# Two chained sequence-model blocks on one Trainium2 core: full tile shapes and two small projections as small tiles, with the first units and the start of the second block reworked

## The chip, the core and the metric

One core of a Trainium2 chip runs the whole program in one launch. The metric is device time in microseconds (us), the median of several executions. TensorE (PE) multiplies, VectorE (DVE), ScalarE (ACT) and GpSimd (POOL) work elementwise, and SyncE (SP) issues the DMA transfers. All data is float32. "fp32r" is float32 rounded so that the TensorE takes it in one pass; a plain float32 matmul is taken in two passes and shows as two records in the trace.

## The reference

The input x has 256 tokens of width 1024. It goes through two blocks, one behind the other.

```python
def first_block(x, ...):
    h = rmsnorm(x, mix_pre_norm[l])
    u = h @ w_in[l]
    u_z, u_xbc, u_dt, u_ly, u_lx, u_g = jnp.split(u, list(IN_SPLITS), axis=-1)
    y_a = ssd_mixer(u_z, u_xbc, u_dt, ...)      # Mamba-2, 16 heads; u_dt has 16 columns
    y_b = rglru_mixer(u_ly, u_lx, ...)
    g = jax.nn.sigmoid(u_g.reshape(b, s, N_BRANCHES, D_MODEL) + gate_b[l])
    merged = g[:, :, 0, :] * (y_a @ w_proj_ssm[l]) + g[:, :, 1, :] * (y_b @ w_proj_lru[l])
    x = x + rmsnorm(merged @ w_out[l], mix_post_norm[l])
    h = rmsnorm(x, ffn_pre_norm[l])
    up = causal_dwconv(h @ w_ffn_up[l], ffn_conv_w[l], ffn_conv_b[l])
    f_gate, f_val = jnp.split(up, 2, axis=-1)
    f = (jax.nn.gelu(f_gate, approximate=True) * f_val) @ w_ffn_down[l]
    return x + rmsnorm(f, ffn_post_norm[l])

def _layer(x, mem, ...):                        # the second block
    h = _rmsnorm(x, norm_pre)
    cols = h @ w_in
    (dn_qkv, dn_z, dn_b, dn_a, gm_uv, gm_z, sw_q, sw_k, sw_v, sw_z,
     xm_q, xm_z, gate_logits) = _split_cols(cols)   # dn_b and dn_a have 4 columns each
    mem_kv = _rmsnorm(mem, norm_mem) @ w_mem_kv
    y_a = _deltanet_branch(dn_qkv, dn_z, dn_b, dn_a, ...)
    y_b = _spatial_gating_branch(gm_uv, gm_z, ...)
    y_c = _sliding_window_branch(sw_q, sw_k, sw_v, sw_z, sinks)   # 8 heads of 64, 2 key heads
    y_m = _memory_branch(xm_q, xm_z, mem_kv)
    ...
    merged = jnp.sum(gates * proj, axis=2)
    return x + _rmsnorm(merged @ w_out, norm_post)
```

## The kernel before

**Weights.** Each weight is streamed from memory in 260 units of 128x1024 (512 KB), in the order of the list that `stream` builds. SP fetches a unit into one of NR = 5 raw buffers. ACT copies it, rounded, to WH (`split` in the ACT program, L1230). DVE makes the rest, WL = raw - WH (L1741). There are NS = 4 pairs of WH and WL. The activations are split in the same way into a high part (Hh, or YBh) and a low part (Hl, or YBl). PE does three products for each 128x128 piece of a weight: high by high, high by low, low by high (`three`, L605 to L607). The names t_wh, t_wl, t_hh, t_hl and t_br in the trace are these buffers (t_br holds YBh and YBl in turn with other data), and L610 (`mm`) is every other matmul.

**Chunks.** `chunk` (L625) multiplies 256 columns of a weight, two units with 24 matmuls of 256 tokens each. `turned` and `four` keep the tokens on the partitions, and write 512 weight columns with one matmul. `chunk_by_k` goes over the 8 parts of the activations one at a time and waits for each.

**Order.** Every engine's program walks through the same units (`Walk`, L194). At each unit a tick goes by, at which the side work, called lanes, is stepped on: the scan of the SSD branch, the recurrence, the chain of the second block's deltanet (`dn_lane`), its sliding window (`sw_lane`), and others. A lane waits with `walk.until(t)` for a tick out of a table such as T_SW (L301). So the order on each engine is fixed, and a late operation holds up what stands behind it. `bank_table` (L251) says which of the 8 PSUM banks each chunk writes.

**Start.** SP fetches unit 0, the parameters (par), x in four pieces, the constants (con), units 1 to 4, then masks and block matrices (bd). ACT makes the high part of x times the norm's weight (YBh), and DVE the low part (YBl). PE begins with "dt", a chunk of 128 columns of which 16 are wanted, then sums the squares of x over the partitions with a column of ones (`column_sums`, L715), then xbc4, the spread of the norm over the partitions (`norm_spread`), and xbc5. These run on x before the norm; g0 and xbc0 behind them need the normed Hh and Hl.

**Between the blocks.** The last column tile of the first block's FFN (j = 23) passes ACT, then a rounded copy of it is made and its low part on POOL (L2454). Its matmuls are the last ones of the down projection. `sqrt_table` (L1270) loads another set of ACT's functions. Chunks mk2 and mk3 of the memory's keys and values run on PE while the FFN's output is normed, turned by PE (`tr`, L613) and split again. The second block's units begin with "dn_ba", a chunk of 128 columns of which 8 are wanted, and dnq.

**Sliding window.** For each of 4 x 2 steps a visit to PE makes the scores S (a mask in bf16, then queries by keys, on tiles of 64 rows by 64 heads' channels), and a later one the output o (probabilities by values, 64 output columns). The visits stand between the 512-wide matmuls of the gates' chunks.

## Time and profile before

| what | value |
| --- | --- |
| runs | 869.72, 871.77, 869.59 us |
| median | 869.72 us |
| the profiled execution's own time | 871.67 us |
| its span in the trace | 869.8 us |
| granted TensorE clock, mean | 0.995 |
| busy: PE, DVE, ACT, POOL | 848.3, 624.1, 509.0, 78.4 us |
| DMA | 149.21 MB, mean 172 GB/s |

The span runs from the first to the last event in the trace; the profiled execution took 1.87 us more than its span. The median of the runs is 1.95 us under the profiled execution. "Busy" counts the time in which an engine had an instruction in work. PEld is the loading of weights into the TensorE, which overlaps its matmuls.

### The profile page before, as it was taken

How to read it: one execution, taken by the hardware profiler on the slowest of the kernel's cores; microseconds unless marked ns; L12 is line 12 of the kernel's file. 1: busy time of each engine (PE TensorE's matmuls, PEld its weight loads, DVE VectorE, ACT ScalarE, POOL GpSimd, SP SyncE). 2: the span in 40 equal slices, each digit the busy share in tenths (PEclk: the TensorE clock that was granted, in tenths of full speed). 3: DMA queues.
4: the chain of work that ended last, by engine and by line, in shares of the span. 5: the costliest groups of instructions: out<-in, count | busy, mean ns of one | idle time of the engine just before them, and what ended most of it. 6: DMA issues, size and time to landing. Idle time of an engine off the chain costs nothing.

```text
span 869.8 us, 14548 instructions
## 1 busy us (share of the span) xinstructions
PE 848.3 (98%) x5760; PEld 776.0 (89%) x5760; DVE 624.1 (72%) x1124; ACT 509.0 (59%) x826; POOL 78.4 (9%) x83
## 2 busy tenths in 40 slices
PE   5999999999999999999999999999999999999997
PEld 5999999899989999999998799899899887778885
DVE  6787987988868766666665979777555467775765
ACT  5655778665367755555656787554544445544453
POOL 0200001201020111111112100500000100000000
PEclk9999999999999999999999999999999999999999
DMA  9457443466454655555554463844322243365541
GB/s 342 140 190 286 160 140 119 150 211 256 155 199 150 238 188 194 174 182 202 176 194 169 146 198 124 308 147 146 97 98 97 98 145 122 125 213 191 196 145 49
DMA packets 40588, 149.21 MB, mean 172 GB/s; under 512 B 4524, under 2 KB 4680, under 8 KB 39880
## 3 DMA queue, kind: packets, MB, share of 16 engines
q1 hardware_dynamic: 40520, 148.27, 50.2%
q8 instruction: 46, 0.75, 0.3%
q14 instruction: 22, 0.18, 0.1%
HBM read 147.18 MB, written 1.08 MB: 170 GB/s over the span
## 4 chain that ended last, share of the span: by engine, by line
PE 87%; DVE 7%; ACT 3%; issue 2%; DMA 1%; SPq 0%; DVEq 0%; ACTq 0%
PE bank L610 39%; PE bank L605 16%; PE bank L607 15%; PE bank L606 15%; PE bank L613 2%; DVE t_wl L1741 2%; DVE t_arena L1756 1%; DVE t_arena L1746 1%; ACT t_arena L1235 1%; DVE t_x L1756 1%; ACT t_hh L1235 1%; DMA t_x<-in_xin 1%; ACT t_wh L1230 1%; DVE t_sm L1753 1%; ACT t_br L1235 0%
## 5 line engine op out<-in xcount | busy, mean ns | idle before, releaser
L1741 DVE TENSOR_TENSOR t_wl<-t_raw,t_wh 128x1024 fp32r<-128x1024 f32 x260 | 316.6, 1226 | 112.1 <-ACT t_wh L1230 111.0
L1230 ACT ACTIVATE t_wh<-t_raw 128x1024 fp32r<-128x1024 f32 x260 | 273.4, 1058 | 128.3 <-PE bank L610 60.6
L605 PE MATMUL bank<-t_hh,t_wh 128*128 128x256 f32 x1144 | 330.3, 289 | 2.9 <-DVE t_hl L1746 1.5
L607 PE MATMUL bank<-t_hh,t_wl 128*128 128x256 f32 x1144 | 323.5, 283 | 0.0
L606 PE MATMUL bank<-t_hl,t_wh 128*128 128x256 f32 x1144 | 323.5, 283 | 0.0
L605 PEld LDWEIGHTS bank<-t_hh,t_wh 128*128 128x128 f32 x1144 | 219.1, 192 | 6.8 <-issue 4.2
L606 PEld LDWEIGHTS bank<-t_hl,t_wh 128*128 128x128 f32 x1144 | 219.2, 192 | 0.8
L607 PEld LDWEIGHTS bank<-t_hh,t_wl 128*128 128x128 f32 x1144 | 219.1, 191 | 0.0
L610 PE MATMUL bank<-t_wh,t_br 128*128 128x512 f32 x384 | 123.5, 392 | 0.2 <-POOL t_br L2454 0.2
L1756 DVE SCALAR_TENSOR_TENSOR t_arena<-bank,t_par,t_arena 128x255 f32<-128x255 f32 (+2 forms) x184 | 75.2, 474 | 45.0 <-ACT t_arena L1235 44.7
L610 PE MATMUL bank<-t_wh,t_hh 128*128 128x512 f32 x224 | 91.9, 410 | 1.8 <-DVE t_wl L1741 1.8
L610 PE MATMUL bank<-t_wh,t_hl 128*128 128x512 f32 x224 | 88.3, 394 | 0.0
L610 PE MATMUL bank<-t_wl,t_hh 128*128 128x512 f32 x224 | 88.2, 394 | 0.0
L610 PEld LDWEIGHTS bank<-t_wh,t_br 128*128 128x128 f32 x384 | 72.2, 188 | 16.2 <-issue 1.6
L1235 ACT ACTIVATE t_arena<-bank 128x512 f32<-128x512 f32 (+4 forms) x75 | 42.2, 575 | 62.0 <-PE bank L610 35.5
L610 PE MATMUL bank<-t_wl,t_br 128*128 128x512 f32 x192 | 74.9, 390 | 0.0
L2454 POOL TENSOR_TENSOR t_br<-t_arena,t_br 128x256 fp32r<-128x256 f32 x30 | 34.5, 1154 | 307.5 <-ACT t_br L1235 307.5
L1235 ACT ACTIVATE t_arena<-bank,t_par 128x256 f32<-128x256 f32 x76 | 37.6, 547 | 39.3 <-PE bank L607 39.3
L610 PE MATMUL bank<-t_arena 128*128 128x128 f32 (+5 forms) x360 | 54.5, 298 | 0.8 <-DVE t_arena L1746 0.8
L610 PEld LDWEIGHTS bank<-t_wh,t_hh 128*128 128x128 f32 x224 | 42.5, 190 | 12.6 <-DVE t_wl L1741 2.5
L610 PEld LDWEIGHTS bank<-t_arena 128*128 128x128 f32 (+2 forms) x360 | 45.2, 185 | 6.8 <-issue 2.9
L610 PEld LDWEIGHTS bank<-t_wh,t_hl 128*128 128x128 f32 x224 | 42.5, 190 | 9.4
(154 smaller groups left out, 850.3 us busy)
## 6 DMA issues: line engine op xcount, KB each, us to landing
t_raw<-in_ws SPq DMA_DIRECT2D x260, 512.0 KB, 3.9
t_br<-decay SPq DMA_DIRECT2D x1, 2048.0 KB, 8.4
t_arena<-in_post SPq DMA_DIRECT2D x3, 512.0 KB, 4.9
t_arena<-gates SPq DMA_DIRECT2D x1, 1536.0 KB, 10.6
t_x<-in_xin SPq DMA_DIRECT2D x4, 256.0 KB, 5.9
t_bd<-in_bd SPq DMA_DIRECT2D x1, 1024.0 KB, 11.6
t_x<-in_xtok SPq DMA_DIRECT2D x1, 1024.0 KB, 5.8
t_arena<-in_mem SPq DMA_DIRECT2D x1, 1024.0 KB, 8.1
```

The lines of the kernel that those rows point to most:

```text
L605: e.matmul(o, wh, xh, start=first, stop=False, skip_group_check=True)
L606: e.matmul(o, wh, xl, start=False, stop=False, skip_group_check=True)
L607: return e.matmul(o, wl, xh, start=False, stop=last, skip_group_check=True)
L610: return e.matmul(o, l, r, start=st, stop=sp, skip_group_check=True)
L613: return e.transpose(o, i, ident[0:i.shape[0], 0:i.shape[0]])
L1230: e.activation(WH[q % NS][:, :], RAW[q % NR][:, :], ACT.Copy, bias=0.0, scale=1.0).then_inc(*hi.now(q))
L1235: return e.activation(o, i, f, bias=bias, scale=scale)
L1741: e.tensor_tensor(WL[q % NS][:, :], RAW[q % NR][:, :], WH[q % NS][:, :].bitcast(F), SUB).then_inc(*lo.now(q))
L1746: return e.tensor_tensor(o, a, b, op)
L1753: return e.tensor_scalar(o, a, s1, s2, op0, op1)
L1756: return e.scalar_tensor_tensor(out=o, in0=a, scalar=s, in1=b, op0=op0, op1=op1)
L2454: return e.tensor_tensor(o, a, b, op)
```

## The change

- "dt" and "dn_ba" leave the stream, which has two units fewer. Their wanted columns come as small tiles by transfers of their own (`first`, with the first norm's weights, and `gates`). The tile holds high and low weights side by side, 32 columns for dt and 16 for the gates, so each of the 8 parts takes two matmuls: 16 in place of 24, on 32 or 16 columns in place of 128.
- At the start SP issues `first`, x in two pieces, unit 0, the first 280 columns of con, unit 1, par, and then the units; what is left of con, the masks and bd come at units 6, 10 and 12. Constants that POOL made now come from the host. PE runs 5 float32 matmuls on zeros before its first data.
- The squares of x are added on DVE to one tile (two more additions), and so are those of mem and of the SSD's output (two tiles to one in each group). The column sums take 4 records in place of 16 for x and for mem, and 8 in place of 16 for the SSD. Those of x stand inside xbc4, the spread inside xbc5. The root of the first norm comes from ACT with a Newton step on DVE, not from DVE's integer code. g0 is taken unit by unit.
- The chunks pl0 to pl3 wait for each quarter of YB where they need it, no longer for the whole of it ahead of pl0.
- For j = 23 the low part is made on DVE, and `sqrt_table` stands behind the high copy. The FFN's output is turned by tiles of 128 tokens (`turn_tile`), vu's four units come first in the second block, by tiles of tokens, then the small gates tile, then dnq. The deltanet's lane starts 4 to 5 ticks later.
- In the sliding window the keys are laid into a tile with zeros (SWK2, cleared by POOL), so that S uses all 128 rows, and o is made for both key heads at once, on 128 output columns.

The core of the diff:

```diff
-    s.append(("dt", "w_in", rng(DTC, 128)))
...
         s.append((f"dnq{i}", "w_in_2", rng(DNQ + 256 * i, 256)))
-    for n in range(2):
-        for i in range(2):
-            s.append((("vu", "vv")[n] + str(i), "moving", ("w_in_2", i, rng(GMU + 512 * n, 512))))
+    for i in range(2):
+        s.append((f"vv{i}", "moving", ("w_in_2", i, rng(GMU + 512, 512))))
     for i in range(2):
         s.append((f"xmq{i}", "w_in_2", rng(XMQ + 256 * i, 256)))
     for i in range(2):
...
+        SWQt, SWK2 = ar(12, 4, T), ar(58, 2, T)
...
 
+            e.dma_start(DTW, first).then_inc(s_first, 16)
+            for i in range(2):
+                e.dma_start(X[:, 4 * i:4 * i + 4, :], xin[:, 4 * i:4 * i + 4, :]).then_inc(s_x[i], 16)
             fetch(0)
+            e.dma_start(conT[:, 0:NFIRST], con[:, 0:NFIRST]).then_inc(s_con, 16)
+            fetch(1)
             e.dma_start(parT[:, :], par).then_inc(s_par, 16)
-            for i in range(4):
-                e.dma_start(X[:, 2 * i:2 * i + 2, :], xin[:, 2 * i:2 * i + 2, :]).then_inc(s_x[i], 16)
-            e.dma_start(conT[:, :], con).then_inc(s_con, 16)
-            for q in range(1, NR):
+            for q in range(2, NR):
...
-            e.dma_start(MSK, masks).then_inc(s_msk, 16)
-            e.dma_start(bdT[:, :, :], bd).then_inc(s_bd, 16)
             for q in range(NR, NU):
+                if q == 6:
...
+            def turn_tile(tt):
+
+                e.wait_ge(*a_ns.of("scaled", "pre2", tt, 0))
+                e.wait_ge(*d_ns.of("scaled", "pre2", tt, 1))
+                if tt == 0:
+                    for b in (0, 3):
+                        bank_free(("turn", "pre2", b))
+                for k in range(8):
+                    m = tr(PB[TILE_BANK[tt][k // 4]][:, 128 * (k % 4):128 * (k % 4) + 128], XS[:, tt, 128 * k:128 * k + 128])
+                m.then_inc(*p_ht.now("pre2", tt))
+
...
+            def mix_sums():
+                e.wait_ge(s_con, 16)
+                e.wait_ge(*d_add.of("mix", 3))
+                column_sums(7, 0, [SC0[:, 0, :]], True, True).then_inc(*p_norm.now("mix", "sum"))
...
-                    m = column_sums(3, 2 * g, [SSQ[:, 4 * g + k, :] for k in range(2)], g == 0, g == 1)
+                    m = column_sums(3, 2 * g, [SSQ[:, 4 * g, :]], g == 0, g == 1)
...
+                    kt, q = SWK2[:, a_, :], SWQt[:, i, :]
                     yield from walk.until(T_SW[n][0])
...
-                    mm(o[:, 0:T], SWV_[:, 0, r], pt[:, 0:T], True, False)
-                    mm(o[:, 128:T], SWV_[:, 1, r], pt[:, T:384], False, True).then_inc(*p_sw.now("o", i, a_))
+                    mm(PB[6][:, 0:T], SWV_[:, 0, :], pt[:, 0:T], True, False)
+                    mm(PB[6][:, 128:T], SWV_[:, 1, :], pt[:, T:384], False, True).then_inc(*p_sw.now("o", i, a_))
                 yield
 
...
-            chunk_by_k("dt", YBh, YBl, x_weighted)
-            e.wait_ge(s_con, 16)
-            norm_sums_first("mix", 7, SC0)
-            norm_sums_last("mix", 7, SC0)
-            chunk("xbc4", YBh, YBl)
-            norm_spread("mix", 7)
-            chunk("xbc5", YBh, YBl)
+            e.wait_ge(*d_const.of("warm"))
+            for _ in range(5):
+                mm(PB[3][:, 0:T], SC1[:, 0, 0:128], SC1[:, 0, :])
+            e.wait_ge(*d_dt.of("w"))
+            for k in range(8):
+                e.wait_ge(*d_xw.of(k))
+                mm(PB[6][0:32, 0:T], DTS[:, k, :], YBh[:, k, :], k == 0, False)
+                m = mm(PB[6][0:16, 0:T], DTS[:, k, 0:16], YBl[:, k, :], False, k == 7)
+            m.then_inc(*p_dt.now("dt"))
+            chunk("xbc4", YBh, YBl, {(1, 4): mix_sums})
...
-                    chunk_by_k("g0", Hh, Hl, normed("mix"))
-                    e.wait_ge(*d_f.of("mix", 7))
+                    chunk_by_units("g0", Hh, Hl, normed("mix"))
...
 
 
-            e.wait_ge(*d_yb.of(3))
+            def hidden(q):
+                return lambda: e.wait_ge(*d_yb.of(q))
+
             for i in range(4):
-                chunk(f"pl{i}", YBh, YBl)
...
-            norm_sums_first("mem", 3, MEMQ)
-            norm_sums_last("mem", 3, MEMQ)
+            mem_sums()
...
-                    e.wait_ge(*g_fl.of(20 + i))
+                    e.wait_ge(*(d_fp.of("low") if i == 3 else g_fl.of(20 + i)))
...
-                        turn_rows("pre2", 0)()
+                        turn_tile(0)
                     for tt in range(2):
-                        if i == 1 and j == 1 and tt == 1:
...
-            chunk_by_k("dn_ba", Hh, Hl, normed("pre2"))
+            turn_tile(1)
+            us = walk.four(4)
+            for tt in range(2):
+                for i, u in enumerate(us):
+                    if tt == 0:
+                        split_ready(u)
+                    e.wait_ge(*d_hl.of("pre2", tt, 2 * i + 1))
+                    m = turned(f"vu{i // 2}", u, 2 * i, Hh, Hl, i == 0, i == 3, (tt,))
+                    if tt == 1:
+                        m.then_inc(*unit.now(u))
+                if tt == 0:
+                    m.then_inc(*p_tok.now("vu1"))
+            e.wait_ge(*d_rw.of("w"))
+            e.wait_ge(*a_ev.of("free", "vu", 0))
+            for k in range(8):
+                mm(PB[6][0:16, 0:T], BAS[:, k, :], Hh[:, k, :], k == 0, False)
+                m = mm(PB[6][0:8, 0:T], BAS[:, k, 0:8], Hl[:, k, :], False, k == 7)
+            m.then_inc(*p_rw.now("ba"))
...
@@ -1274,11 +1343,47 @@
                 e.wait_ge(*d_ns.of(tag, tt, "rs"))
                 act(XS[:, tt, halves(0)], XT[:, tt, halves(0)], ACT.Copy, scale=row_stats(1, tt)[1]).then_inc(*a_ns.now("scaled", tag, tt, 0))
 
+            def tile_parts(tt, ks):
+                for k in ks:
+                    act(Hh[:, k, 128 * tt:128 * tt + 128], PB[TILE_BANK[tt][k // 4]][:, 128 * (k % 4):128 * (k % 4) + 128], ACT.Copy,
+                        scale=pc("pre2", k)).then_inc(*a_hh.now("pre2", tt, k))
+
+            def second_norm(q):
...
+                e.wait_ge(*p_ht.of(pre, 0))
+                tile_parts(0, range(6))
+                walk.ahead(q + 6)
+                chunk_done("mk3")
+                e.wait_ge(*d_hl.of(pre, 0, 5))
+                tile_parts(0, (6, 7))
+                walk.ahead(q + 7)
+                e.wait_ge(*p_ht.of(pre, 1))
+                tile_parts(1, range(8))
+                act(BAS[:, :, 0:8], BAW, ACT.Copy).then_inc(*a_rw.now("w"))
+
             def token_norm(post, pre, q, between):
...
                     act(cg, cg, ACT.Gelu_apprx_tanh).then_inc(*a_fg.now(j))
-                    if j == 23:
-                        sqrt_table()
...
                     elif j == 0:
                         chunk_done("wo1_1")
                     act(YBh[:, j % 8, :], FF[:, j % 2, :], ACT.Copy).then_inc(*a_fh.now(j))
+                    if j == 23:
+                        sqrt_table()
                 for i in range(6):
...
+                act(YBh[:, k, :], X[:, k, :], ACT.Copy, scale=WMIX[:, k:k + 1]).then_inc(*a_xw.now(k))
             split(0)
-            walk.split_to = 1
-            e.wait_ge(s_par, 16)
-            for k in range(8):
-                if k % 2 == 0:
-                    e.wait_ge(s_x[k // 2], 16)
-                act(YBh[:, k, :], X[:, k, :], ACT.Copy, scale=pc("mixpre", k)).then_inc(*a_xw.now(k))
...
+                yield from walk.until(T_FU[23] + 2)
+                e.wait_ge(*a_fh.of(23))
+                tt(YBl[:, 7, :], FF[:, 1, :], YBh[:, 7, :].bitcast(F), SUB).then_inc(*d_fp.now("low"))
...
-                       ADD).then_inc(*d_ssd.now("gsum", g))
+                       ADD).then_inc(*d_ssd.now("gsums", g))
+                    e.wait_ge(*d_ssd.of("gsums", g))
+                    tt(SSQ[:, 4 * g, :], SSQ[:, 4 * g, :], SSQ[:, 4 * g + 1, :], ADD).then_inc(*d_ssd.now("gsum", g))
...
 
-            split(0)
-            walk.split_to = 1
+            e.memset(SM[:, 392:393], 1.0).then_inc(*d_const.now("one"))
+            e.memset(SC1[:, 0, :], 0.0).then_inc(*d_const.now("warm"))
...
+            e.wait_ge(*d_add.of("mix", 1))
+            tt(SC0[:, 0:2, :], SC0[:, 0:2, :], SC0[:, 6:8, :], ADD).then_inc(*d_add.now("mix", 2))
+            e.wait_ge(*d_add.of("mix", 2))
+            tt(SC0[:, 0, :], SC0[:, 0, :], SC0[:, 1, :], ADD).then_inc(*d_add.now("mix", 3))
+            walk.split_to = 2
+            walk.unit(2)
+            o, v, r, t, h = NW[:, 0, 0:2], NW[:, 1, 0:2], NW[:, 2, 0:2], NW[:, 2, 2:4], NW[:, 1, 2:4]
+            e.wait_ge(*p_norm.of("mix", "sum"))
+            ts(v, PB[7][:, 0:2], 1.0 / 1024, MUL, EPS, ADD).then_inc(*d_rs.now("mix", "v"))
+            e.wait_ge(*d_rs.of("mix", "v"))
```

What stands on PE at the start before (t_br is YBh or YBl, the three rows of a part repeat eight times, then the column sums and xbc4):

```order
L605 MATMUL bank<-t_br,t_wh 128x256
L606 MATMUL bank<-t_br,t_wh 128x256
L607 MATMUL bank<-t_br,t_wl 128x256
```

And what stands there now, of which the second and third row repeat eight times:

```order
L630 MATMUL bank<-t_arena 128x256 x5
L630 MATMUL bank<-t_br,t_wh 32x256
L630 MATMUL bank<-t_br,t_wh 16x256
```

The five matmuls on zeros and 16 narrow ones took the place of 24 full ones, and xbc4 follows them at once.

On ACT at the end of the first block's FFN, before (t_br is the high part of j = 23, t_hh x4 the second half of a norm, L1230 the split of a unit):

```order
L1235 ACTIVATE t_arena<-t_arena 128x256
L1235 ACT_TABLE_LOAD
L1235 ACTIVATE t_sm<-t_con 128x1
L1235 ACTIVATE t_br<-t_arena 128x256
L1235 ACTIVATE t_hh<-t_arena 128x512 x4
L1230 ACTIVATE t_wh<-t_raw 128x1024
L1256 ACTIVATE t_arena,t_sm<-bank 128x512 x2
```

The same place now:

```order
L1304 ACTIVATE t_arena<-t_arena 128x256
L1304 ACTIVATE t_br<-t_arena 128x256
L1304 ACT_TABLE_LOAD
L1304 ACTIVATE t_sm<-t_con 128x1
L1304 ACTIVATE t_hh<-t_arena 128x512 x4
L1299 ACTIVATE t_wh<-t_raw 128x1024
L1325 ACTIVATE t_arena,t_sm<-bank 128x512 x2
```

The table load moved behind the copy of j = 23's high part; the rest of the row order is kept.

On PE in a visit of the sliding window, o and a part of the deltanet's work, before (t_pw is the tile of values):

```order
L610 MATMUL bank<-t_arena 128x128 x4
L610 MATMUL bank<-t_px,t_arena 128x256 x2
L610 MATMUL bank<-t_pw,t_arena 64x256
L610 MATMUL bank<-t_pw,t_arena 64x128
L605 MATMUL bank<-t_hh,t_wh 128x256
```

And now:

```order
L630 MATMUL bank<-t_arena 128x128 x4
L630 MATMUL bank<-t_px,t_arena 128x256 x2
L630 MATMUL bank<-t_pw,t_arena 128x256
L630 MATMUL bank<-t_pw,t_arena 128x128
L625 MATMUL bank<-t_hh,t_wh 128x256
```

Nothing moved here; the two matmuls write 128 columns in place of 64.

## Rows read from the trace of the kernel before

**Rows 1.** The page: span, and busy time of each engine.

```profile
span 869.8 us, 14548 instructions
PE 848.3 (98%) x5760; PEld 776.0 (89%) x5760; DVE 624.1 (72%) x1124; ACT 509.0 (59%) x826; POOL 78.4 (9%) x83
```

**Rows 2.** PE's waits: line, releaser, us in total, times, longest.

```profile
PE bank L605 <- DVE t_br L1756: 8.5, 1, 8.5
PE bank L610 <- DVE t_wl L1741: 1.8, 1, 1.8
```

**Rows 3.** Windows: length, PE, PEld, DVE, ACT, POOL, clock, DMA share, GB/s.

```profile
8.53:11.70 3.17, 3.17 (x15) 3.17 (x16) 2.65 (x7) 3.17 (x9) 0.00 (x0) 1.00 1.01 376
15.07:18.50 3.43, 3.43 (x18) 3.43 (x18) 3.29 (x10) 1.58 (x2) 0.00 (x0) 0.51 1.01 418
489.24:493.00 3.76, 3.76 (x10) 2.98 (x11) 3.51 (x12) 3.26 (x5) 0.00 (x0) 0.55 0.42 139
```

**Rows 4.** Timeline of ACT and DVE at the start: start, duration, instruction, wait.

```profile
4.67 1.06 ACT L1230 ACTIVATE t_wh<-t_raw 128x1024 fp32r<-128x1024 f32 x1 [2.66 <-DMA t_raw<-in_ws]
7.36 3.30 ACT L1235 ACTIVATE t_br<-t_x,t_par 128x256 fp32r<-128x256 f32 x8 [1.64 <-DMA t_x<-in_xin]
7.90 3.27 DVE L1756 SCALAR_TENSOR_TENSOR t_br<-t_x,t_par,t_br 128x256 fp32r<-128x256 f32 x8 [0.92 <-ACT t_br L1235]
```

**Rows 5.** Timeline of PE from the column sums to g0.

```profile
13.29 1.92 PE L610 MATMUL bank<-t_con,t_arena 128*128 128x1 f32 x16 [0.25 <-DVE t_arena L1746]
15.07 0.53 PE L605 MATMUL bank<-t_br,t_wh 128*128 128x256 f32 x1
...
30.68 0.36 PE L605 MATMUL bank<-t_hh,t_wh 128*128 128x256 f32 x1 [1.50 <-DVE t_hl L1746]
```

**Rows 6.** Timeline of PE, a visit with full 128-row tiles.

```profile
102.17 0.28 PE L607 MATMUL bank<-t_hh,t_wl 128*128 128x256 f32 x1
102.29 1.03 PE L610 MATMUL bank<-t_arena,t_bd 128*128 128x256 f32 x4
103.27 0.28 PE L606 MATMUL bank<-t_hl,t_wh 128*128 128x256 f32 x1
```

**Rows 7.** Timeline of PE, a visit of the SSD lane with 64-column tiles.

```profile
132.56 0.88 PE L610 MATMUL bank<-t_x,t_arena 128*64 128x256 f32 x8
```

**Rows 8.** Timeline of PE, the sliding window's o and S visits.

```profile
734.20 0.39 PE L610 MATMUL bank<-t_wh,t_hl 128*128 128x512 f32 x1
734.52 0.86 PE L610 MATMUL bank<-t_pw,t_arena 128*64 128x256 f32 x4
735.65 0.40 PE L610 MATMUL bank<-t_wl,t_hh 128*128 128x512 f32 x1
...
737.75 0.39 PE L610 MATMUL bank<-t_wl,t_hh 128*128 128x512 f32 x1
737.98 0.39 PE L610 MATMUL bank<-t_wh,t_hl 128*128 128x512 f32 x1
...
738.48 0.92 PE L610 MATMUL bank<-t_arena 64*128 64x128 f32 x4
...
739.66 0.40 PE L610 MATMUL bank<-t_wl,t_hh 128*128 128x512 f32 x1
```

**Rows 9.** Timeline of PE, pl0's first matmul, and the column sums of mem.

```profile
190.54 0.39 PE L605 MATMUL bank<-t_br,t_wh 128*128 128x256 f32 x1 [0.32 <-DVE t_br L1746]
...
222.09 1.84 PE L610 MATMUL bank<-t_con,t_arena 128*128 128x1 f32 x16
```

**Rows 10.** Timeline between the blocks, ACT, DVE and PE.

```profile
473.34 1.28 ACT L1235 ACT_TABLE_LOAD   x1
...
475.08 2.18 ACT L1235 ACTIVATE t_hh<-t_arena 128x512 fp32r<-128x512 f32 x4
...
487.97 1.22 DVE L1741 TENSOR_TENSOR t_wl<-t_raw,t_wh 128x1024 fp32r<-128x1024 f32 x1
...
489.24 0.53 PE L610 MATMUL bank<-t_wh,t_hh 128*128 128x512 f32 x1 [1.82 <-DVE t_wl L1741]
```

More of the change, by code:

```diff
@@ L326, in dn_bank, with build_program @@
     return 3 + (DN_AT[name] + 1) % 3
-def build_program(nc, ws, par, con, masks, bd, rows, swt, xin, xtok, min_, post, decay, gates2, out):
+def build_program(nc, first, gates, ws, par, con, masks, bd, rows, swt, xin, xtok, min_, post, decay, gates2, out):
     ctx = ExitStack()
@@ L641, in chunk, with chunk_by_units @@
                     walk.tick()
+            def chunk_by_units(name, xh, xl, x_ready):
+                b = BANK[name]
+                for j in range(2):
+                    q = walk.unit(NS - 1 - j)
+                    wh, wl = weights(q, 8)
+                    split_ready(q)
+                    if j == 0:
+                        bank_free(name)
+                    for k in range(8):
+                        if j == 0:
+                            x_ready(k)
+                        m = three(half(b, j), wh[:, k, :], wl[:, k, :], xh[:, k, :], xl[:, k, :], k == 0, k == 7)
+                    m.then_inc(*unit.now(q))
             def chunk_by_k(name, xh, xl, x_ready):
@@ L1630, in act_program @@
                 act(MV[:, tt, :], PB[BANK["mv", tt]][:, :], ACT.Copy).then_inc(*a_ev.now("free", "mv", tt))
-            walk.cols("dn_ba", True)
+            walk.four(4)
+            for tk in range(2):
+                e.wait_ge(*tokens_done("vu1", tk))
+                act(GU[:, tk, :], PB[BANK["vu", tk]][:, :], ACT.Gelu_apprx_tanh).then_inc(*a_ev.now("free", "vu", tk))
+                walk.ahead(FIRST["dnq0"] + 2)
             for i in range(6):
@@ L1669, in act_program @@
             chunk_done("swkv")
-            act(SWK_[:, 0, :], half(BANK["swkv"], 0), ACT.Copy)
+            e.wait_ge(*g_dn.of("pads"))
+            for a in range(2):
+                act(SWK2[64 * a:64 * a + 64, a, :], half(BANK["swkv"], 0)[64 * a:64 * a + 64, :], ACT.Copy)
             act(SWVt[:, 0, :], half(BANK["swkv"], 1), ACT.Copy).then_inc(*a_ev.now("swkv"))
@@ L2279, in dve_program @@
-            square_adds("mix", SC0)
-            walk.cols("dt", True)
-            rsqrt("mix", NW, 7, 2, 1024, p_norm.of("mix", "sum"))
-            walk.cols("xbc4")
-            e.wait_ge(*p_norm.of("mix", "row"))
+                stt(YBl[:, k, :], X[:, k, :], WMIX[:, k:k + 1], YBh[:, k, :].bitcast(F), MUL, SUB).then_inc(*d_xw.now(k))
+            split(0)
+            e.wait_ge(*a_sq.of("mix", 1))
+            tt(SC0[:, 0:2, :], SC0[:, 0:2, :], SC0[:, 2:4, :], ADD).then_inc(*d_add.now("mix", 0))
@@ new lines, in dve_program @@
+            walk.split_to = 2
+            walk.unit(2)
+            o, v, r, t, h = NW[:, 0, 0:2], NW[:, 1, 0:2], NW[:, 2, 0:2], NW[:, 2, 2:4], NW[:, 1, 2:4]
+            e.wait_ge(*p_norm.of("mix", "sum"))
+            ts(v, PB[7][:, 0:2], 1.0 / 1024, MUL, EPS, ADD).then_inc(*d_rs.now("mix", "v"))
+            e.wait_ge(*d_rs.of("mix", "v"))
+            ts(h, v, -0.5, MUL).then_inc(*d_rs.now("mix", "half"))
+            e.wait_ge(*a_sq.of("mix", "root"))
+            e.reciprocal(o, r).then_inc(*d_rs.now("mix", "guess"))
@@ L2284, in dve_program @@
+            e.wait_ge(*d_rs.last())
+            tt(t, o, o, MUL).then_inc(*d_rs.now("mix", "oo"))
+            e.wait_ge(*d_rs.last())
+            tt(t, t, h, MUL).then_inc(*d_rs.now("mix", "t"))
+            e.wait_ge(*d_rs.last())
+            stt(o, t, 1.5, o, ADD, MUL).then_inc(*d_rs.now("mix"))
+            walk.tick()
+            walk.unit(2)
+            walk.tick()
+            walk.unit(1)
+            walk.tick()
+            h_parts("mix", SC1, X, WMIX, 7, {4: 4})
             e.tensor_copy(ROWR, PB[7][:, 0:T]).then_inc(*d_const.now("row"))
-            walk.cols("xbc5")
@@ L2286, in dve_program @@
-            h_parts("mix", SC1, X, "mixpre", 7)
+            e.wait_ge(s_par, 16)
+            walk.unit()
+            walk.tick()
             ts(hbr, pc("br", 0, 8), 0.5, MUL)
@@ L2370, in dve_program @@
             walk.four(3)
[L2371 removed]
+            second_norm(FIRST["mk2"])
             walk.cols("mk2", True)
             walk.cols("mk3")
[L2376 removed]
+            walk.four(4)
             for i in range(6):
@@ L2548, in pool_program @@
             walk.tick()
-            walk.cols("pl0")
-            block_masks()
-            for i in range(1, 4):
+            for i in range(4):
                 walk.cols(f"pl{i}")
@@ L2572, in pool_program @@
             walk.cols("mk3")
-            walk.cols("dn_ba", True)
+            walk.four(4)
             for name in MIDDLE:
```

361 lines of the change are left out of this document (222 added, 139 removed).

## The prediction

> **What bounds the kernel now.** I read the page first. PE has an instruction in work for 848.3 of 869.8 us, DVE for 624.1 and ACT for 509.0 [rows 1], so the time is PE's instructions one behind the other, and an edit is worth what it takes off PE or off PE's few waits. The list of PE's waits comes next: one of 8.5 us before the first matmul and one of 1.8 us at a t_wl are the largest [rows 2]; the timeline shows 1.50 us ahead of g0 [rows 5] and 0.32 us at pl0 [rows 9]. Then the windows: the granted clock is 0.51 from 15.07 to 18.50 us and 0.55 from 489.24 to 493.00, the 1.2 GHz level, and 1.00 elsewhere. The engine worked through the 6.5 us before the first of these and stood still before the second [rows 3]. In 3.43 us at 0.51 PE got through 18 matmuls, 0.19 us each. At full clock a matmul on 256 columns follows the last after 0.12 us (102.17 to 102.29 [rows 6]) and one on 512 columns after 0.23 us (737.75 to 737.98 [rows 8]). These are the prices of the sum.
>
> **Part A, the start.** Before, ACT splits unit 0 at 4.67, waits 1.64 us for x, and makes YBh in 3.30 us, 0.41 us for each of the 8 parts; the low parts on DVE end half a microsecond later (11.17) [rows 4]. The dt matmuls run from 8.53 and are done at about 13; the sums of squares follow, and xbc4 starts at 15.07 [rows 5]. After, x is no longer queued behind unit 0 and par. Half a megabyte at 376 to 418 GB/s [rows 3] takes 1.3 us, so x comes some 1.5 to 2 us earlier, and YBh starts at about 5.5. It ends at 5.5 + 3.3 = 8.8, the split of unit 0 at 8.8 + 1.06 = 9.9, and DVE's part of it at 9.9 + 1.22 = 11.1; with the squares' additions between, I put xbc4 at 11.5. The 16 narrow dt matmuls keep ACT's pace and are done before. The matmuls on zeros run while PE would wait.
>
> xbc4 has 48 matmuls (48 x 0.12 = 5.8 us) and now 4 records of column sums (rows 9 give 1.84 / 16 = 0.115 us for a record, so 0.5): it ends at 17.7. xbc5 takes 5.8 and the spread 0.4, so PE could begin g0 at 23.9. The norm must be through by then. Its sums stand in xbc4 three quarters of the way, at about 16; root, reciprocal and Newton step are some ten small operations, the spread follows, and the normed parts can begin at about 19.8. Hh and Hl are made at 0.4 to 0.5 us a part, with two splits between: about 24.0. So the 1.50 us wait goes. In its second unit g0 waits for DVE, which has Hl and the splits queued, about 0.9 us. g0 ends at 24.0 + 5.8 + 0.9 + 0.4 = 31.1, where before it ended at 30.68 + 5.8 = 36.5. That is 5.4 us. DVE then stands closer to PE than before: its work up to unit 20 is the same and PE is 5 us nearer, so I give back 0.9 to 2.5 us and take **-3.7 us** (bounds -5.5 and -2.5; if a stretch at 1.2 GHz falls into xbc4 as it does now, it costs 1.7 us as it did).
>
> **Part B, sums and small waits.** For mem 12 records go and for the SSD's groups 8, 20 x 0.115 = 2.3 us on PE's path. In exchange DVE gets additions of 256 columns that lie beside PE's work. pl0's wait of 0.32 us [rows 9] goes, since its first matmuls need only a quarter of YB. Together **-2.6 us** (bounds -2.0 and -3.0, the low one if DVE's additions push pl0's later quarters).
>
> **Part C, full shapes in the sliding window.** From 734.20 to 735.65 lie two 512-wide intervals and one o visit: 1.45 - 2 x 0.23 = 0.99 us. From 737.98 to 739.66 likewise 1.68 - 0.46 = 1.22 us for an S visit [rows 8]. What a visit with full tiles costs stands at 102.17 to 103.27: 1.10 - 2 x 0.12 = 0.86 us for two matmuls of 256 columns, four records, and nothing beyond them, 0.215 a record [rows 6]. The o visit has 256 and 128 columns in two passes, 3 x 0.215 = 0.65: it saves 0.34. The S visit has the same two and a mask of 384 bf16 columns (0.23 x 384 / 512 = 0.17): 0.82, it saves 0.40. Eight of each are 8 x 0.74 = 5.9; two o visits share their place with other narrow tiles, which keeps a tenth: **-5.8 us** (bounds -4.5 and -6.3). The price of cleared keys (a POOL write) and of one more copy on ACT lies far from PE's path: both engines are idle for much of the span.
>
> What the saving rests on is that a narrow tile brings a cost around it, and that narrow tiles do not overlap each other. The SSD lane's visit speaks against the second: eight records on 64 columns in 0.88 us [rows 7], as long as four in the o visit at 0.86 [rows 8], so pairs on different columns ran side by side there. In the sliding window the two matmuls of a step use one tile, one after the other, and nothing stands beside them; so the full shape gives up no overlap. The Trainium skill says the same of the cost around ("TensorEngine Tiling (Array Packing)", Key Properties: "Mode switching requires drain"). But another of its rules speaks against the edit: "TensorE: Matmul & The Clock Gate", Part 3, has small tiles run concurrently, and advises slicing them so. By that rule alone the 64-row tiles were no slower than full ones, and part C would be 0.
>
> **Part D, the start of the second block.** What goes: dn_ba, 24 x 0.12 = 2.9 us and a short wait and pacing around it, 0.4 together. What comes: 16 narrow matmuls, 16 x 0.115 = 1.8, and a visit's extra of 0.34 as in part C. Net -1.1 us. vu's four units only move. The chain on ACT that ends at the first matmul of the second block is made longer. The table load of 1.28 us stays ahead of the four Hh copies (2.18 us) [rows 10], it only passes behind j = 23's high copy, which PE needs: PE is done with the FFN earlier and then waits for mk2 and mk3 that much longer, a gain of nothing. For mk3 the split at 487.97 must still be done before PE goes on at 489.24 [rows 10]. New are 16 copies by halves of the tokens in place of 8, and the cast of the gates' tile, some 1.5 us on ACT, of which vu on the first tile hides part only. I take +1.6 for these, and **D = +0.5 us** (bounds -2 and +3.5; a stretch at 1.2 GHz more or less is 1.7 us either way, which is what 489.24 to 493.00 costs now: 3.76 x 0.45 [rows 3]). The deltanet's lane starts 4 to 5 ticks later; it had some 16 ticks to spare before its output is wanted, so I cost it at nothing. What covers it are the gates' chunks. Without that cover, each tick is a unit of some 2.8 us.
>
> **Sum.** -3.7 - 2.6 - 5.8 + 0.5 = -11.6. Against the profiled execution's 871.67 us this is 860.1; the median of the runs is 1.95 lower, which gives 858.1. I say **858.2 us**, and its own range is 854 to 862.
>
> **The rivals.**
> 1. The start brings little: the work on DVE up to unit 20 decides, not PE's order. For it: at 0.51 clock DVE was busy 3.29 of 3.43 us [rows 3]. Against: masks, bd and 24 matmuls do leave the start. Then A is -1 and the time 861.
> 2. The second block's start loses: two more waits of 1.5 us, and a second stretch at 0.55. D is +3.5 and the time 861.
> 3. Full shapes bring nothing, either by the rule of concurrent tiles or because the 0.3 us around a narrow visit belongs to any float32 visit. Against: the visit at 102 us [rows 6] is such a one and has nothing around it. The time is 864.
> 4. On the other side: the deltanet's chain becomes what PE waits for. It is fixed in order; if it comes 5 ticks late and its slack is gone, PE's waits are those of its steps, about 45 visits x 0.3 us = 13.5 us, less the 11.6, so 871.6 on the median. It decides from 11.6 us on. For it: the lane was moved. Against: PE waits 1.1 us in two places for t_arena in all, so nothing is near the edge today.
> 5. Both the start and the second block gain in full, and no stretch at 1.2 GHz falls into xbc4 or vu: A -5.5, D -2, 853.
>
> **How the numbers follow.** The forecast 0.62, rival 1 0.12, rival 2 0.12, rival 3 0.07, rival 4 0.02, rival 5 0.05. The range 853.5 to 863.5 holds the forecast and rivals 1 and 2 with their neighbours and leaves out most of 3 to 5. 0.3% is 2.6 us, about what a measurement tells from no change. Faster takes all but rival 4 and a part of mixed mishaps: 0.95; the same 0.03; slower 0.02.
>
> **What would show it.** In the changed kernel's timeline: xbc4 at about 11.5 and g0 at about 24 with no wait ahead of it, xbc0 at about 31; column sums of 4 records; o visits of 0.65 us and S visits of 0.82 between 512-wide matmuls; at pl0 no wait; in the windows the stretches at half clock; ahead of vu waits of 1 to 2 us for a split or an Hl. I am wrong if the visits keep 0.99 and 1.22 us, if DVE sets the first 50 us, or if PE's waits for t_arena grow over some microseconds.

## The result, and the profile after

The changed kernel took 863.94 us in the median (863.07 to 866.02, 4 runs), the kernel before 870.55 us beside it. The ratio is 0.9927, with a 95% interval of 0.9902 to 0.9952: 0.5 to 1.0% faster. The forecast was 858.2 us with a range of 853.5 to 863.5. The direction holds, the gain is 6.6 us where 11.6 were worked out, and the median lies just above the range.

The page of the changed kernel:

```profile
span 864.2 us, 14493 instructions
PE 840.4 (97%) x5726; PEld 772.3 (89%) x5726; DVE 625.4 (72%) x1130; ACT 510.9 (59%) x839; POOL 72.8 (8%) x76
```

PE's busy time fell by 7.9 us against [rows 1], although 4.0 us of matmuls on zeros are new in it; the span fell by 5.6. The list of PE's waits answers to [rows 2]:

```profile
PE bank L633 <- DVE t_arena L1871: 3.3, 2, 1.7
PE bank L630 <- DVE t_wl L1866: 3.2, 2, 1.6
PE bank L625 <- DVE t_wl L1866: 2.6, 4, 1.4
PE bank L630 <- DVE t_px L1881: 2.4, 1, 2.4
PE bank L630 <- DVE t_arena L1871: 1.7, 1, 1.7
PE bank L630 <- DVE t_br L1881: 1.4, 1, 1.4
```

The wait of 8.5 us at the start is down to 1.4, since PE now has its matmuls on zeros there (1.2 us of waiting stand ahead of them and 1.4 us ahead of xbc4); but t_arena and t_px stand for 3.3 + 2.4 + 1.7 = 7.4 us in four places, where the kernel before had one wait above a quarter of a microsecond of this kind (0.8). The timeline of PE from the start to the middle (start, duration, instruction, wait):

```profile
1.21 3.99 PE L630 MATMUL bank<-t_arena 128*128 128x256 f32 x10 [1.21 <-DVE t_arena L2439]
11.12 0.51 PE L625 MATMUL bank<-t_br,t_wh 128*128 128x256 f32 x1 [1.43 <-DVE t_wl L1866]
48.97 0.39 PE L625 MATMUL bank<-t_hh,t_wh 128*128 128x256 f32 x1 [0.35 <-DVE t_wl L1866]
216.34 0.50 PE L630 MATMUL bank<-t_con,t_arena 128*128 128x1 f32 x4
483.37 0.51 PE L630 MATMUL bank<-t_wh,t_hh 128*128 128x512 f32 x1 [1.64 <-DVE t_wl L1866]
```

The place at 48.97 is this one of the kernel before:

```profile
52.97 0.38 PE L605 MATMUL bank<-t_hh,t_wh 128*128 128x256 f32 x1 [0.36 <-DVE t_wl L1741]
```

So the start is worth 4.0 us. xbc4 starts at 11.12, 3.95 us sooner than in [rows 5]. At the column sums of mem the lead is 222.09 - 216.34 = 5.75 us, against [rows 9], and behind them 7.1, since 4 records stand for 16. At mk3 it is 489.24 - 483.37 = 5.9 us, against [rows 10]: 1.2 us were lost between the blocks. The four visits in which PE now waits:

```profile
568.33 0.45 PE L630 MATMUL bank<-t_px,t_arena 128*128 128x256 f32 x1 [2.36 <-DVE t_px L1881]
662.69 0.55 PE L633 MATMUL bank<-t_con,t_arena 128*128 128x128 f32 x3 [1.66 <-DVE t_arena L1871]
684.72 0.49 PE L630 MATMUL bank<-t_arena 128*128 128x128 f32 x2 [1.72 <-DVE t_arena L1871]
756.57 0.66 PE L633 MATMUL bank<-t_con,t_arena 128*128 128x128 f32 x4 [1.60 <-DVE t_arena L1871]
```

The first is the spatial gating's product at tick 171, the others are the deltanet's transposes at tick 193, its product at 197, and its last transposes at 214. Of the first one's 2.36 us about 1 us belongs to this one execution: in the traces of `xm1`, `table_back` and `no_warm` below, whose edits lie elsewhere, that wait is 1.41, 1.44 and 1.39 us, so the four are 6.4 us without it. A fifth, of 0.86 us at 637 us for ACT, is new as well and stands for the 0.8 that went. What DVE does ahead of the second of the four:

```profile
652.64 0.17 DVE L1877 TENSOR_SCALAR t_sm<-t_sm 128x2 f32<-128x2 f32 x1
656.59 0.17 DVE L2392 RECIPROCAL t_sm<-t_sm 128x2 f32<-128x2 f32 x1 [3.77 <-ACT t_px L1583]
...
657.32 0.61 DVE L2418 TENSOR_REDUCE t_sm<-bank 128x1 f32<-128x128 f32 x2
657.97 0.23 DVE L1878 TENSOR_SCALAR t_sm<-t_sm 128x2 f32<-128x2 f32 x1
659.36 0.16 DVE L1871 TENSOR_TENSOR t_sm<-t_sm 128x2 f32<-128x2 f32 x1 [1.16 <-ACT t_sm L1304]
...
660.82 1.21 DVE L1866 TENSOR_TENSOR t_wl<-t_raw,t_wh 128x1024 fp32r<-128x1024 f32 x1
661.96 1.27 DVE L1871 TENSOR_TENSOR t_arena<-t_arena,bank 128x512 f32<-128x512 f32 x2
```

This is tick 191: the softmax of the memory attention's last head (t_px) and one of the sliding window (t_pw) stand one behind the other, each with a wait for ACT's exponential, then a unit's low part, and only then the sum (t_arena) for which PE waits. Between 652.64 and 661.96 us DVE waited twice, for 3.77 and 1.16 us, so it was not short of time. What held PE up was the order of the work. The longer wait goes back to PE itself, by way of ACT: the exponential stands on ACT behind a copy of the deltanet's product, and that copy waited for PE:

```profile
655.05 0.60 ACT L1304 ACTIVATE t_arena<-bank 128x512 f32<-128x512 f32 x1 [3.40 <-PE bank L630]
```

In the kernel before, ACT has done the deltanet's copies by then (from 665.26 us), and DVE's wait at the same softmax is 1.09 us.

The windows that answer to [rows 3], the first columns as there:

```profile
11.12:14.58 3.46, 3.46 (x16) 3.46 (x17) 3.16 (x5) 2.66 (x4) 0.00 (x0) 0.52 1.06 414
483.37:487.00 3.63, 3.63 (x19) 3.04 (x20) 3.42 (x13) 2.80 (x5) 0.00 (x0) 1.00 0.49 158
```

In this execution the stretch at the lower clock near the start is still there, and the one at 489 us is gone.

### The profile page after: what moved, and what is told of

Read it like the earlier page. It is cut to its first block and busy times, and to the rows that moved or that the text cites. A ratio compares the mean times of both kernels' runs of the same rounds, so it can differ in the third digit from the quotient of the medians.

```text
span 864.2 us, 14493 instructions
## 1 busy us (share of the span) xinstructions
PE 840.4 (97%) x5726; PEld 772.3 (89%) x5726; DVE 625.4 (72%) x1130; ACT 510.9 (59%) x839; POOL 72.8 (8%) x76
## 5 line engine op out<-in xcount | busy, mean ns | idle before, releaser
L1304 ACT ACTIVATE t_arena<-bank 128x512 f32<-128x512 f32 (+5 forms) x76 | 42.7, 572 | 54.5 <-PE bank L630 35.5
L630 PE MATMUL bank<-t_arena 128*128 128x128 f32 (+4 forms) x370 | 57.7, 304 | 2.9 <-DVE t_arena L1871 1.7
L630 PEld LDWEIGHTS bank<-t_arena 128*128 128x128 f32 (+2 forms) x370 | 48.8, 189 | 8.3 <-DVE t_arena L1871 2.1
```

The costliest lines, as they stand in the source:

```text
L630: return e.matmul(o, l, r, start=st, stop=sp, skip_group_check=True)
L1304: return e.activation(o, i, f, bias=bias, scale=scale)
```

## The experiments

Each ratio is to the kernel before, run beside it. Times that are compared with the changed kernel's 863.94 were measured apart from it and are good to about 1 us: the kernel before, run beside each, moved between 869.65 and 871.51 us. Where a trace shows the same thing, its number stands beside.

**The sliding window's shapes, alone and undone.** `sw_only` is the kernel before with

```diff
-                    kt, q = SWK_[r, 0, :], SWQt[r, i, :]
+                    kt, q = SWK2[:, a_, :], SWQt[:, i, :]
...
-                    mm(o[:, 0:T], SWV_[:, 0, r], pt[:, 0:T], True, False)
-                    mm(o[:, 128:T], SWV_[:, 1, r], pt[:, T:384], False, True)
+                    mm(PB[6][:, 0:T], SWV_[:, 0, :], pt[:, 0:T], True, False)
+                    mm(PB[6][:, 128:T], SWV_[:, 1, :], pt[:, T:384], False, True)
```

and the cleared SWK2; `sw_undone` is the changed kernel with the reverse.

> The kernel before with the full shapes in the sliding window and nothing else of the change. If the visits are worth what the prediction priced (8 x 0.34 and 8 x 0.40 us), the span falls by 5 to 6 us, to about 864. If the saved time only turns into waits for DVE behind it (PE arrives sooner, DVE does not), it falls by less than 3 us and new waits of 1 us and more show between 600 and 790 us.

> The changed kernel with the narrow tiles (64 rows in S, 64 columns in o) put back. If the new waits at about 565, 661, 683 and 755 us come from where the deltanet's steps stand, all four stay and the span grows by 5 to 6 us. If they come from the faster sliding window, the three after 600 us shrink and the span grows by less than 3 us.

Measured: `sw_only` 866.33 us, ratio 0.9946 (0.9930 to 0.9963), 5.2 us faster than its 871.51 beside it. `sw_undone` 869.41, 5.5 us above the changed kernel (4.5 by the ratios, 0.9979 against 0.9927), and with all four waits. The first is 1.46 us, as in the other traces with this program, the second and third 1.66 and 1.73 as there, and the last is 0.65 where it was 1.60. An o visit and an S visit of the changed kernel, in the timeline of PE:

```profile
741.77 0.39 PE L630 MATMUL bank<-t_wh,t_br 128*128 128x512 f32 x1
742.00 0.81 PE L630 MATMUL bank<-t_pw,t_arena 128*128 128x256 f32 x4
742.57 0.47 PE L630 MATMUL bank<-t_wh,t_br 128*128 128x512 f32 x1
742.88 0.39 PE L630 MATMUL bank<-t_wl,t_br 128*128 128x512 f32 x1
...
745.17 0.39 PE L630 MATMUL bank<-t_wh,t_br 128*128 128x512 f32 x1
745.40 0.34 PE L630 MATMUL bank<-t_maskW,t_identB 128*128 128x384 bf16 x1
745.58 0.82 PE L630 MATMUL bank<-t_arena 128*128 128x128 f32 x4
...
746.47 0.40 PE L630 MATMUL bank<-t_wl,t_hh 128*128 128x512 f32 x1
```

The o visit with its two neighbours takes 742.88 - 741.77 = 1.11 us, where [rows 8] have 1.45: 0.34 saved. The S visit takes 746.47 - 745.17 = 1.30, where [rows 8] have 1.68: 0.38. Part C was priced rightly, and its gain comes through in both surroundings. Three of the four waits are not the faster window's. Of the last one 0.95 us is: it is 0.65 and 0.66 us with the narrow tiles (`sw_undone`, `shift_only`) and 1.60 with the full ones, so in the changed kernel about 1 us of what the visits save is given back there.

**The deltanet's lane one tick earlier.** `dn4` is the changed kernel with every tick of that lane from 185 on lowered by 1 (185 + 3 * level to 184 + 3 * level, and so on, on all engines), `dn4_gm` the same with

```diff
-                    yield from walk.until(171 + gp)
+                    yield from walk.until(172 + gp)
```

> The changed kernel with the deltanet's steps from tick 185 on one tick earlier, so that the whole lane stands 4 ticks later than before, not 5; the sliding window and the memory attention have a pattern of 4 ticks. Theory of the phase (a step's addition on DVE falls behind both softmaxes of the same tick): the waits at about 661, 683 and 755 us go, some 4 to 5 us, span about 860 where the changed kernel's was 864.2. Theory of the load (DVE has too much in this stretch, wherever it stands): waits come back elsewhere and the span changes by less than 1.5 us. The wait at 566 us stays in both.

> As the last one, and the spatial gating's two matmul steps one tick later (172, 173). Theory: the wait of 2.4 us at 568 us is PE at tick 171 waiting for a norm that DVE begins at tick 169 behind the deltanet's transposed values, which the change moved there; a tick is 2.9 us of PE's work, so the wait goes and the span falls by a further 2 us and more, to about 858. If DVE is simply late there, the wait only moves by a tick.

Measured: `dn4` 867.98 us (0.9971, 0.9956 to 0.9985), `dn4_gm` 867.65. Both are some 4 us slower than the changed kernel. The theory of the phase fell: the three waits went, but two larger ones came. The list of PE's waits of `dn4`:

```profile
PE bank L630 <- DVE t_arena L1871: 3.6, 1, 3.6
PE bank L633 <- DVE t_arena L1871: 3.0, 1, 3.0
```

and a window behind the first of them, where the clock fell as well:

```profile
661.48:665.00 3.52, 3.52 (x18) 3.30 (x19) 1.68 (x2) 0.60 (x1) 0.00 (x0) 0.67 0.62 193
```

Behind the second, from 753.48 to 757.00 us, it was 0.69. The waits grew by 1.6 us on balance (6.6 for the 5.0 that went), and these stretches are a further part of the 4 us. Of the theory stays what its timeline shows: DVE's work of tick 191 is the same two softmaxes, and the step that has its due time next behind them waits. With the lane 5 ticks late it is the sum for tick 193; with 4 it is the masked copy for tick 193, which DVE makes behind the softmaxes; before the change the next step was due two ticks later. The spatial gating's wait went in `dn4_gm`, as expected.

**The double tick parted.** `xm1` moves only the memory attention's last head:

```diff
-T_XM = [(175, 177, 182), (183, 185, 186), (187, 189, 190), (191, 193, 194)]
+T_XM = [(175, 177, 182), (183, 185, 186), (187, 189, 190), (192, 194, 195)]
```

> The changed kernel with the memory attention's last head one tick later (192, 194, 195), the deltanet left where it is. At tick 191 DVE does the softmax of that head and one of the sliding window; in this theory, whatever step of the deltanet is due on PE soonest behind that tick waits for it (before the change that step came two ticks later). Expected: the wait at about 661 us (1.8 us) goes, the other three stay, span down by 1 to 2 us. If DVE's load and not the double tick makes it, the wait stays, since the same work stands between.

Measured: 862.75 us (0.9918, 0.9904 to 0.9933), 1.2 us under the changed kernel. In its trace the wait at 662 us is gone, the one at 684 us is 2.06 us in place of 1.72, and the other two stay. The same work in another order takes the wait away.

**Four places loosened.** `sp2` is the changed kernel with

```diff
-T_SW = [(179, 181, 190)] + [(191 + 4 * n, 193 + 4 * n, 194 + 4 * n) for n in range(7)]
+T_SW = [(179, 181, 190)] + [(192 + 4 * n, 194 + 4 * n, 195 + 4 * n) for n in range(7)]
...
-                    yield from walk.until(193 + 3 * n)
+                    yield from walk.until(193 + 4 * n)
...
-                yield from walk.until(214)
+                yield from walk.until(216)
...
-                    yield from walk.until(171 + gp)
+                    yield from walk.until(172 + gp)
```

where the deltanet's ticks between 193 and 214 go with the second line (194 and 195 + 4 * n, then 200, 203, 204).

> The changed kernel with four places loosened: the spatial gating's matmuls one tick later, the sliding window from its second step one tick later, the deltanet from the second of its two block steps one tick later, and its last transposes a tick later still. If the missing 8 us are waits between lanes that meet on DVE at a tick, all four go and the span is about 857 (864.2 less 6 to 8). If DVE is short of time there, waits of the same sum show up at other steps, and the span falls by less than 2 us.

Measured: 856.82 us (0.9854, 0.9840 to 0.9869), 7.1 us under the changed kernel, and 6.4 by the ratios (0.9927 less 0.9854), which is what the four waits sum to in the other traces (1.4 + 1.66 + 1.72 + 1.60). PE's waits on L1871 and t_px are no longer in its list, though the deltanet's lane ends a tick or two later still:

```profile
PE bank L630 <- DVE t_wl L1866: 3.2, 2, 1.6
PE bank L625 <- DVE t_wl L1866: 2.6, 4, 1.4
PE bank L630 <- DVE t_arena L2439: 1.2, 1, 1.2
```

**The lane's shift alone.** `shift_only` is the kernel before with the changed kernel's ticks in the deltanet's lane, and nothing else:

```diff
-                    yield from walk.until(161 + hf)
+                    yield from walk.until(165 + hf)
...
-                yield from walk.until(209)
+                yield from walk.until(214)
```

> The kernel before with one part of the change alone: the deltanet's lane on all engines at the changed kernel's ticks (4 later, 5 later from tick 180), everything else as before. If the waits come from the lane's new place alone, the kernel before gets them too: about 2 us at the spatial gating's matmuls, and 1.8 us at each of three later steps, 6 to 8 us in all, span 876 to 878. If they need the reordered start of the second block, or PE's lead from the first block, the span stays within 2 us of 869.8.

Measured: 878.06 us against 870.99, ratio 1.0082 (1.0065 to 1.0099), 7.1 us slower. Its waits:

```profile
PE bank L613 <- DVE t_arena L1746: 2.3, 2, 1.7
PE bank L610 <- DVE t_arena L1746: 2.1, 2, 1.7
PE bank L610 <- DVE t_px L1756: 1.9, 1, 1.9
PE bank L613 <- ACT t_arena L1235: 0.9, 1, 0.9
```

The waits come from the lane's place alone; the last one, at the deltanet's last transposes, is 0.66 us here and not 1.8, as said above. The new waits behind 500 us sum to 6.8 us, less the 0.8 that went. PE falls back by 7.3 us in that stretch; the other 1.3 us are in no wait above a quarter of a microsecond and were not traced.

**The table load put back.** `table_back` has `sqrt_table()` for j = 23 ahead of the wait and the copy again:

```diff
                     act(cg, cg, ACT.Gelu_apprx_tanh).then_inc(*a_fg.now(j))
+                    if j == 23:
+                        sqrt_table()
...
                     act(YBh[:, j % 8, :], FF[:, j % 2, :], ACT.Copy).then_inc(*a_fh.now(j))
-                    if j == 23:
-                        sqrt_table()
```

> The changed kernel with the load of ACT's table for the square root where it was, ahead of the high copy of the last column tile. The prediction held the move to be worth nothing, since ACT does the same work up to the second half's norm either way. Then PE's last matmuls of the down projection start 1.3 us later, its two waits at 476 and 481 us are 1.3 us shorter in all, and the span is the same within 0.5 us. If the move did help, the span grows by over 1 us.

Measured: 861.93 us (0.9916, 0.9900 to 0.9933), 2.0 under the changed kernel (1.0 by the ratios). Neither expected outcome came: the move had cost time. The noise of a microsecond has its part in the 2.0; the traces are clearer. ACT in the changed kernel:

```profile
465.81 0.42 ACT L1304 ACTIVATE t_arena<-t_arena 128x256 f32<-128x256 f32 x1 [0.38 <-DVE t_arena L1881]
467.67 0.42 ACT L1304 ACTIVATE t_br<-t_arena 128x256 fp32r<-128x256 f32 x1 [1.44 <-DVE t_arena L1871]
468.10 1.28 ACT L1304 ACT_TABLE_LOAD   x1
```

and in `table_back`:

```profile
464.26 0.42 ACT L1304 ACTIVATE t_arena<-t_arena 128x256 f32<-128x256 f32 x1 [0.38 <-DVE t_arena L1881]
464.70 1.28 ACT L1304 ACT_TABLE_LOAD   x1
465.99 0.20 ACT L1304 ACTIVATE t_sm<-t_con 128x1 f32<-128x1 f32 x1
466.11 0.42 ACT L1304 ACTIVATE t_br<-t_arena 128x256 fp32r<-128x256 f32 x1
```

Between the gelu and the copy ACT waits 1.44 us for DVE. Where the load stood before, it filled that wait; behind the copy it is added to the chain. Of PE's two waits of 1.6 us for t_wl, at 479 and 483 us, the first is gone in `table_back`. mk3 starts at 480.30 us in `table_back` and at 481.68 in `sp2`, whose start took the same time: 1.4 us.

**The matmuls on zeros left out.** `no_warm` is the changed kernel without the loop over five matmuls.

> The changed kernel without the five float32 matmuls on zeros at the start. The prediction gave them no term. If they only fill time in which PE would wait, the span is the same. If the clock falls in another place or time for their lack, the first 20 us differ: the narrow matmuls of dt and the first half of xbc4 would then run at the lower clock, up to 2 us more, and no stretch at 0.5 would follow within xbc4.

Measured: 863.42 us (0.9930), the same as the changed kernel. PE's first narrow matmul starts at 6.61 us, and its windows row for the first half of xbc4 is

```profile
11.00:14.58 3.58, 3.58 (x17) 3.58 (x17) 3.28 (x5) 2.66 (x4) 0.00 (x0) 1.00 1.03 414
```

17 matmuls in 3.58 us, 0.21 each as at 1.2 GHz, though the granted clock reads 1.00. In the changed kernel it is 16 in 3.46 at 0.52. The stretch of 3.5 us at the lower pace stands in the same place, by either way; in `sp2`'s trace it is absent, and its g0 comes 1.7 us sooner. No run shows a gain from the zeros: three executions of `no_warm` took 863.35 to 863.43 us, the two fastest of the changed kernel 863.07 and 863.25.

**x behind unit 0.**

```diff
+            fetch(0)
             for i in range(2):
                 e.dma_start(X[:, 4 * i:4 * i + 4, :], xin[:, 4 * i:4 * i + 4, :]).then_inc(s_x[i], 16)
-            fetch(0)
```

> The changed kernel with x queued behind unit 0 again. By the prediction's working x then lands 1.3 us later (half a megabyte at some 400 GB/s), the high and low parts of x with it, and the end of g0 comes 1.3 us later at the most. The rival (DVE's queue sets the first 50 us): the 1.3 us are lost in DVE's slack and the span is the same.

Measured: 867.4 us (0.9963, 0.9949 to 0.9976), 3.5 above the changed kernel. ACT's first part of x starts at 8.37 us where it was 5.39, 3.0 later and not 1.3:

```profile
8.37 3.30 ACT L1304 ACTIVATE t_br<-t_x,t_arena 128x256 fp32r<-128x256 f32 x8 [5.47 <-DMA t_x<-in_xin]
```

The DMA view of the changed kernel over its first 12 us, in 40 slices of 0.3 us:

```profile
GB/s 0 0 0 0 0 25 187 102 109 150 232 273 314 300 410 382 382 328 341 287 314 300 246 273 253 234 331 449 423 427 436 350 395 429 434 443 410 410 437 410
```

Up to 4 us, in which x is on its way, it moves 25 to 314 GB/s; a steady 400 comes only after 8. At the 188 GB/s that the slices from 1.5 to 4.2 us show on average, half a megabyte takes an estimated 2.8 us. The working took the price of later for the start. The rival fell: nothing of it is lost in DVE's slack. In this trace, which has no stretch at the lower clock, PE comes to the place that was at 48.97 at 50.31 us, in `sp2`'s, which has none either, at 47.30: 3.0 us.

**Column sums and pl0's wait undone.** `sums_back` has the second pair of tiles in each sum again, without DVE's additions, and pl0 waits for all of YB:

```diff
-                    m = column_sums(3, 2 * g, [SSQ[:, 4 * g, :]], g == 0, g == 1)
+                    m = column_sums(3, 2 * g, [SSQ[:, 4 * g + k, :] for k in range(2)], g == 0, g == 1)
...
-            mem_sums()
+            norm_sums_first("mem", 3, MEMQ)
+            norm_sums_last("mem", 3, MEMQ)
```

> The changed kernel with 12 more column-sum records for mem, 8 more for the SSD's output, without DVE's additions for them, and with pl0 waiting for the whole of YB again. The prediction's part B says +2.6 us (20 x 0.115 and 0.3); the trace of the changed kernel has PE 3.4 us further ahead at 495 us than at 49 us, which would make it +3.4. If DVE's additions cost something elsewhere, less.

Measured: 867.18 us (0.9956, 0.9940 to 0.9973), 3.2 above the changed kernel, 2.5 by the ratios. Behind both sums the same matmul of PE, in the changed kernel and in `sums_back`:

```profile
265.42 0.33 PE L633 MATMUL bank<-t_con,t_arena 128*128 128x128 f32 x1 [0.34 <-DVE t_wl L1866]
268.37 0.33 PE L633 MATMUL bank<-t_con,t_arena 128*128 128x128 f32 x1 [0.34 <-DVE t_wl L1867]
```

Of these 2.95 us 0.1 was there at 49 us already, so part B is worth 2.9.

**The best of it.** `best` is `sp2` with the edit of `table_back`.

> The loosened places of sp2 and the table load where it was before the change (table_back), together. Each alone gave about 7 and 1.5 to 2 us against the changed kernel; they lie 80 us and more apart, so they should add: 855 to 856 us, 14 to 15 us under the kernel before. If the wait that the early table load filled comes back between the blocks once the second block runs tighter, it is no better than sp2's 856.8.

Measured: 856.92 us (855.38 to 857.35), ratio 0.9839 (0.9824 to 0.9854). Its median is `sp2`'s. Its profiled execution had the slow stretch near the start (0.68 from 10 to 15 us) and `sp2`'s had not, and both spans are 854.9. Like for like the table's 1.4 us are there: mk3 starts at 481.85 us, and at 483.37 in the changed kernel, which had the stretch too. The median can't show them.

## Why the prediction was right and wrong

| part | predicted | found | where |
| --- | --- | --- | --- |
| A, start | -3.7 | -4.0 | 52.97 to 48.97 us |
| B, sums, pl0 | -2.6 | -2.9 in the trace, -3.2 | `sums_back` |
| C, full shapes | -5.8 | -5.2, -5.5 | `sw_only`, `sw_undone` |
| D, second block's start | +0.5 | about +5.6 | the rest of -6.6; below |

- **Part A** was right in its sum and in xbc4's start (11.12 for 11.5) by terms that were not all right. x costs 3.0 us behind a unit, not 1.3; that the working had "some 1.5 to 2 us" and came close with "at about 5.5" (5.39) was luck in part, since x came in quarters before and comes in halves now. The wait ahead of g0 went: g0 starts at 25.83 us, and at 24.16 in `sp2` without the stretch at 1.2 GHz, for "about 24.0". The stretch fell into xbc4 as before.
- **Part B** was right, 0.3 us short. The lead of 7.1 us behind mem's sums holds a further 0.3 that is not part B's: a wait for t_wl ahead of them fell from 0.73 us (at 159.20 before) to 0.42 (at 154.90), and in `sums_back` it stays at 0.41.
- **Part C** was right to a few hundredths of a microsecond per visit. The rule of concurrent tiles (rival 3) did not take it away: the narrow tiles had run one after the other. A wait behind it took about 1 us in the changed kernel, at the deltanet's last transposes; the working had no term for that.
- **Part D failed, in two steps.** The first is "The deltanet's lane starts 4 to 5 ticks later; it had some 16 ticks to spare before its output is wanted, so I cost it at nothing." No row shows the 16 ticks, but its output was indeed not late: `sp2` ends the lane later still, and no wait comes of it. But a lane is not one work with one due time: each of its steps has a due time of a tick or two, on queues of DVE and ACT that it shares with the other lanes, and those were not moved. 5 ticks later its steps fell behind other lanes' work. It cost four waits of 6.4 us in the other traces with this program (7.4 in the profiled one) and 7.1 us by `shift_only`, and `sp2` gives 6.4 to 7.1 back. The second is "a gain of nothing" for the table load, which lost the cover of ACT's wait for DVE: 1.4 us. Without the first step D would be about -1 (5.6 less 6.4), within its bounds.
- **Rival 4** named the moved lane and gave it 2 in 100. Its price was put on the wrong thing, the end of the chain and all 45 visits; four visits paid 6.4 to 7.4 us. A part of that price, short of the 11.6 us from which the rival decides, was in no case of the list, and so not in the range. "PE waits 1.1 us in two places for t_arena in all, so nothing is near the edge today" read a sum of waits as slack: a wait of zero says nothing about how much was left.
- Of rival 2 a part held (two waits at mk2 and mk3, 3.2 us for 1.8), but without a stretch at 0.55. That it fell away is not the change's doing alone: the trace of `shift_only`, whose program is the kernel before's up to there, has none either. PE came out of that place only 0.6 us sooner for it, since a wait of 0.77 us followed; the 1.7 us that the working had for it is too much.

What stays open: how much of D is vu's new place and the small gates tile. The parts' sum with the four waits at 6.4 us, -4.0 - 2.9 - 5.4 + 6.4 + 1.4 = -4.5, leaves some -2 us for them and for the lower clock at 489 us; no run parts these. The -1.1 us of D's working for the small tile would fit into it, and is not shown.

## What to carry to other kernels

Where several engines' programs interleave side work by a fixed table of ticks, moving one lane against the others is a change to every one of its steps: for each, look at what stands ahead of it on the shared engine at its new tick, above all a round trip to another engine, and not at when its last result is due. A load or a copy that costs nothing may cost nothing because it fills a wait; before it is moved, look at what the next row on its engine waits for. Here four places loosened by a tick or two gave 6.4 to 7.1 us, as much as the whole change.
